# Sums of the gate's modulation moved from the merge stage into the stage of Strassen pairs

## The reference

```python
def modulation(cvec, w_ada, b_ada):
    mod = jax.nn.silu(cvec) @ w_ada + b_ada          # w_ada: 2048 x 6144
    shift, scale, gate = jnp.split(mod[:, None, :], 3, axis=-1)
...
    u = rmsnorm(x, norm_pre_w) * (1 + scale) + shift
    aq, ak, av, az, mq, mk, mv, mo, mz, mg, ga, gb = split_proj(u, w_in)
    ... windowed attention (branch B), mLSTM scans (branch A) ...
    merged = jax.nn.sigmoid(ga) * (y_a @ w_proj_a) + jax.nn.sigmoid(gb) * (y_b @ w_proj_b)
    out = rmsnorm(merged @ w_out, norm_post_w)
    return x + gate * out
```

## Time and profile before

| | |
|---|---|
| time, median of 3 runs | 1955.51 us (1955.37 to 1955.7) |
| the profiled execution: its own time | 1955.12 us |
| its span, first to last instruction | 1953.5 us |
| PE busy | 1920.3 us, 98% |
| DVE busy | 1204.0 us, 62% |
| ACT busy | 668.8 us, 34% |
| POOL busy | 113.2 us, 6% |
| mean granted clock of PE | 0.998 |

### The profile page before, as it was taken

How to read it: one execution, slowest core, us unless ns; L and a number is a source line. 1 busy time by engine, 2 the same in 40 slices (tenths; PEclk the granted TensorE clock), 3 DMA queues, 4 the chain that set the end, 5 groups by cost and what they waited for, 6 DMA issues and landing times.

```text
span 1953.5 us, 31682 instructions
## 1 busy us (share of the span) xinstructions
PE 1920.3 (98%) x12266; PEld 1782.6 (91%) x12266; DVE 1204.0 (62%) x2073; ACT 668.8 (34%) x1017; POOL 113.2 (6%) x201
## 2 busy tenths in 40 slices
PE   6999999999999999999999999999999999999998
PEld 2589999999999999999898999889889999988886
DVE  3368766666666666665766664465557767683224
ACT  4453333333333333332555554233224222242221
POOL 2010000000000000000000000000002000000000
PEclk9999999999999999999999999999999999999999
DMA  9962353333333333334632423355355666633224
GB/s 369 391 197 86 111 164 110 111 112 113 113 113 113 113 113 113 113 113 127 183 109 80 122 75 118 91 150 135 108 130 144 203 203 184 210 116 140 80 76 162
DMA packets 302319, 274.04 MB, mean 140 GB/s; under 512 B 20384, under 2 KB 253608, under 8 KB 300320
## 3 DMA queue, kind: packets, MB, share of 16 engines
q1 hardware_dynamic: 287984, 216.71, 37.9%
q0 software_dynamic: 13952, 56.00, 7.9%
q10 hardware_dynamic: 304, 0.25, 0.0%
HBM read 235.05 MB, written 40.48 MB: 141 GB/s over the span
## 4 chain that ended last, share of the span: by engine, by line
PE 91%; DVE 3%; DMA 3%; ACT 1%; issue 1%; SPq 1%; POOL 0%; DVEq 0%; POOLq 0%; ACTq 0%
PE bank L2060 20%; PE bank L2140 12%; PE bank L2133 12%; PE bank L2134 12%; PE bank L2356 11%; PE bank L2069 10%; PE bank L1973 2%; PE bank L2033 2%; PE bank L2260 2%; PE bank L2249 1%; PE bank L2201 1%; PE bank L2262 1%; PE bank L2178 1%; PE bank L2009 1%; DMA WORK<-in_w_ada_dram 1%
## 5 line engine op out<-in xcount | busy, mean ns | idle before, releaser
L2060 PE MATMUL bank<-XH,WH 128*128 128x320 f32 x1472 | 345.5, 316 | 2.8 <-DVE XL L1847 2.1
L1041 ACT ACTIVATE WH<-RAW 128x1024 fp32r<-128x1024 f32 x195 | 206.7, 1060 | 386.1 <-PE bank L2140 306.2
L2060 PE MATMUL bank<-XL,WH 128*128 128x320 f32 x1472 | 335.1, 309 | 0.0
L1482 DVE TENSOR_TENSOR WL<-RAW,WH 128x1024 fp32r<-128x1024 f32 x195 | 238.3, 1222 | 143.8 <-ACT WH L1041 143.8
L920 ACT ACTIVATE WH<-RAW 128x1024 fp32r<-128x1024 f32 x122 | 129.1, 1059 | 532.3 <-PE bank L2069 407.8
L2060 PEld LDWEIGHTS bank<-XH,WH 128*128 128x128 f32 x1472 | 244.5, 188 | 10.8 <-issue 8.0
L2060 PEld LDWEIGHTS bank<-XL,WH 128*128 128x128 f32 x1472 | 246.2, 188 | 0.0
L2069 PE MATMUL bank<-XH,WL 128*128 128x320 f32 x1472 | 235.9, 310 | 0.0
L2069 PEld LDWEIGHTS bank<-XH,WL 128*128 128x128 f32 x1472 | 220.0, 188 | 4.1 <-issue 3.8
L2134 PE MATMUL bank<-XL,WH 128*128 128x320 f32 x720 | 212.5, 309 | 0.0
L2133 PE MATMUL bank<-XH,WH 128*128 128x320 f32 x720 | 212.5, 309 | 0.0
(11 more groups left out here) (245 smaller groups left out, 2962.9 us busy)
## 6 DMA issues: line engine op xcount, KB each, us to landing
RAW<-in_w_in_dram SPq DMA_DIRECT2D x165, 512.0 KB, 3.8
WORK<-in_w_ada_dram SPq DMA_DIRECT2D x62, 512.0 KB, 5.4
proj_dram<-OUTS POOLq DMA_DIRECT2D x92, 320.0 KB, 2.5
RAW<-in_w_out_dram SPq DMA_DIRECT2D x32, 512.0 KB, 3.9
WORK<-proj_dram SPq DMA_DIRECT2D x16, 640.0 KB, 4.5
WORK<-proj_dram POOLq DMA_DIRECT2D x32, 320.0 KB, 3.3
RAW<-in_w_ada_dram SPq DMA_DIRECT2D x18, 512.0 KB, 9.3
RAW<-in_w_proj_a_dram SPq DMA_DIRECT2D x16, 512.0 KB, 4.7
```

The costliest lines, as they stand in the source:

```text
L1041: ins = nc.scalar.activation(WH[:, (j + p) % 2, :], pair_raw(j, p), ACT.Copy)
L1482: V.tensor_tensor(WL[:, w, :], pair_raw(j, p), WH[:, w, :].bitcast(F32), ALU.subtract)\
L2060: pe.matmul(banks[n][:, 0:HALF_TOK], wh[:, k, :], x[:, k0 + k, n * HALF_TOK:(n + 1) * HALF_TOK], start=(first and k == 0 and wi == 0), sto ...
```

## The change

The gate's sums move into the pair stage. `w_ada` is now taken in 64 pieces of 128 rows (one k-tile) by 512 columns, 256 KB each, loaded by POOL into four buffers (GAR). DVE adds each into GACC, which holds 512 columns for the two vectors: two instructions a step. The 16 steps of one column group fill 8 pairs; POOL then stores GACC to device memory (`gsum`, 512 KB), and the next group starts. Three groups lie in pairs 1 to 24 (two steps a pair); the fourth lies in the last five pairs with 4, 3, 3, 3 and 3 steps. The hardware loops of all engines now hold 8 pairs and run 3 times. In the merge stage SP's loads of `w_ada`, the memset and the 32 steps are gone; POOL loads the four stored sums back into GS, with `norm_post_w` and `b_ada`, and DVE adds `b_ada` to partition 0 in two instructions. WORK grows by 3000 words a partition, and the area of SBUF for the descriptors of POOL's DMAs is set to 4096 bytes a partition. A few semaphores of the start are merged into one (`setup`, and `m0_in` into `scan_in`).

```diff
+LOOP, LOOPS = 8, 3
+GADA_LAST = [4, 3, 3, 3, 3]
+assert 1 + LOOP * LOOPS + len(GADA_LAST) == PAIRS and sum(GADA_LAST) == KT
+WORK_WORDS = 14500
...
+    gsum = nc.dram_tensor("gsum_dram", (4 * P, 2 * 512), F32, kind="Internal").ap()
...
+        GACC = WORK[:, 11400:12424].rearrange("p (v n) -> p v n", v=2)
+        GAR = WORK[:, 12424:14472].rearrange("p (s n) -> p s n", s=4)
...
+        def gada_steps(j):
+            if j <= LOOP * LOOPS:
+                return range(2 * ((j - 1) % LOOP), 2 * ((j - 1) % LOOP) + 2)
+            n = j - LOOP * LOOPS - 1
+            return range(sum(GADA_LAST[:n]), sum(GADA_LAST[:n + 1]))
...
@@ SP, merge stage
-                        gada_load(i, 2 * k + x)
...
@@ POOL, pair stage
+            def gada_store(i, m):
+                pool.wait_ge(gada_used, 16 * i + 16 * (m + 1))
+                pool.dma_start(gsum[bass.ds(P * i + P * m, P), :], GACC.rearrange("p v n -> p (v n)")).then_inc(gacc_out, 16)
+                pool.wait_ge(gacc_out, 16 * i + 16 * (m + 1))
+                nc.gpsimd.tensor_tensor(ZERO[:, 7:8], ZERO[:, 0:1], ZERO[:, 0:1], ALU.add).then_inc(gacc_free, 1)
+            def gada_loads(i, m, steps):
+                for k in steps:
+                    if m or k >= 4:
+                        pool.wait_ge(gada_used, 16 * i + (16 * m + k - 3))
+                    pool.dma_start(GAR[:, k % 4, :], w_ada[0, k * P:(k + 1) * P, bass.ds(512 * i + 512 * m + 4096, 512)])\
+                        .then_inc(gada_in[k % 4], 16)
...
-            with pool.Fori(1, PAIRS_PLAIN // 2) as i:
-                for j in (1, 2):
-                    spill_pair(i, j, 4 * i + (T_PAIR + 2 * j + 2))
+            with pool.Fori(1, LOOPS) as i:
+                for j in range(1, LOOP + 1):
+                    if j < LOOP:
+                        gada_loads(i, 0, gada_steps(j + 1))
+                    else:
+                        gada_loads(i, 1, range(2))
+                        gada_store(i, 0)
+                    spill_pair(i, j, 2 * LOOP * i + (T_PAIR + 2 * j + 2))
+            for j in range(LOOP * LOOPS + 1, PAIRS):
+                if j == LOOP * LOOPS + 1:
+                    gada_loads(0, 3, range(2, GADA_LAST[0]))
+                if j + 1 < PAIRS:
+                    gada_loads(0, 3, gada_steps(j + 1))
+                else:
+                    gada_store(0, LOOPS)
+                spill_pair(0, j, T_PAIR + 2 * j + 2 if j < PAIRS_PLAIN else RB_GA + 2 * (j - PAIRS_PLAIN))
...
@@ POOL, merge stage
-            nc.gpsimd.memset(GS, 0.0).then_inc(filled, 1)
-            pool.wait_ge(filled, 4)
-            for v in range(2):
-                pool.dma_start(GS[0:1, v, :], b_ada[0:1, 4096:6144]).then_inc(gacc_init, 16)
+            pool.wait_ge(gacc_out, 16 * 4)
+            for m in range(4):
+                pool.dma_start(GS[:, :, 512 * m:512 * m + 512],
+                               gsum[m * P:(m + 1) * P, :].rearrange("p (v n) -> p v n", v=2)).then_inc(gs_in, 16)
+            pool.dma_start(NPW, norm_post_w[0].partition_broadcast(P)).then_inc(gs_in, 16)
+            pool.dma_start(GBIAS, b_ada[0:1, 4096:6144]).then_inc(gs_in, 16)
...
@@ DVE, pair stage
+            def gada_step(i, j, k):
+                m = 0 if j <= LOOP * LOOPS and not (isinstance(i, int) and j > LOOP) else LOOPS
+                dve.wait_ge(gada_in[k % 4], 64 * i + (64 * m + 16 * (k // 4 + 1)))
+                if k == 0:
+                    dve.wait_ge(gacc_free, i + (m + 1))
+                else:
+                    dve.wait_ge(gada_used, 16 * i + (16 * m + k))
+                for v in range(2):
+                    acc = GACC[:, v, :]
+                    col = VC[:, k + 16 * v:k + 16 * v + 1]
+                    if k == 0:
+                        ins = V.tensor_scalar(acc, GAR[:, 0, :], col, None, ALU.mult)
+                    else:
+                        ins = V.scalar_tensor_tensor(acc, GAR[:, k % 4, :], col, acc, ALU.mult, ALU.add)
+                ins.then_inc(gada_used, 1)
...
                 pair_lo(i, j, PR_S2)
...
+                if steps:
+                    gada_step(i, j, steps[0])
                 pair_lo(i, j, PR_S1)
...
                     pair_lo(i, j, PR_S3)
+                    gada_step(i, j, steps[1])
                     pair_lo(i, j, PR_S4)
+                    for k in steps[2:]:
+                        gada_step(i, j, k)
                 sums_b(i, j)
...
-            with dve.Fori(0, PAIRS // 2 - 1) as i:
-                for j in (1, 2):
+            with dve.Fori(0, LOOPS) as i:
+                for j in range(1, LOOP + 1):
...
@@ DVE, merge stage
-                    gada_step(i, 2 * u)
                     lo(i, 4, 2 * (T_MERGE + u) + 3)
-                    gada_step(i, 2 * u + 1)
...
+            dve.wait_ge(gs_in, 16 * 6)
+            for v in range(2):
+                ins = V.tensor_tensor(GS[0:1, v, :], GS[0:1, v, :], GBIAS, ALU.add)
+            ins.then_inc(gs_bias, 1)
...
@@ PE, pair stage
-            with pe.Fori(0, (PAIRS - 1) // 2) as i:
-                for j in (1, 2):
+            with pe.Fori(0, LOOPS) as i:
+                for j in range(1, LOOP + 1):
                     for p in range(7):
                         pair_product(i, j, p)
...
-    nc = _bacc.Bacc("TRN2", target_bir_lowering=False, num_devices=1)
+    nc = _bacc.Bacc("TRN2", target_bir_lowering=False, num_devices=1, dynamic_dma_scratch_size=4096)
```

More of the change, by code:

```diff
@@ L386, in hybrid_layer @@
         rows_in, const_in, x_in, aconst_in = sem("rows_in"), sem("const_in"), [sem(f"x_in{b}") for b in range(5)], sem("aconst_in")
-        m0_in, filled = sem("m0_in"), sem("filled")
+        filled = sem("filled")
         raw_in = [sem(f"raw_in{i}") for i in range(4)]
-        gada_in = [sem(f"gada_in{i}") for i in range(2)]
+        gada_in = [sem(f"gada_in{i}") for i in range(4)]
         start_in = [sem(f"start_in{i}") for i in range(START_RAW)]
@@ L565, in _ @@
             pair_pieces(T_PAIR, 0, P * (T_PAIR + 2), False)
[L566 to L571, removed]
+            with sp.Fori(0, LOOPS) as i:
+                for j in range(1, LOOP + 1):
+                    t = T_PAIR + 2 * j
+                    pair_pieces(t, 2 * LOOP * i, 2 * LOOP * P * i + P * (t + 2), j % 2 == 1)
+            for j in range(LOOP * LOOPS + 1, PAIRS):
+                t = T_PAIR + 2 * j
+                pair_pieces(t, 0, P * (t + 2) if j < PAIRS_PLAIN else COL_MERGE + 2 * P * (j - PAIRS_PLAIN), j % 2 == 1)
             def key_loads(g):
@@ L741, in _ @@
                         merge_half(i + 1, k, x)
-                        gada_load(i, 2 * k + x)
[L743 to L746, removed]
+            for q in range(8):
                 out_piece(0, q)
@@ L817, in spill_pair @@
             def spill_pair(i, j, row):
-                pool.wait_ge(sums, 12 * i + (6 * j + 6))
+                pool.wait_ge(sums, 6 * LOOP * i + (6 * j + 6))
                 pool.dma_start(proj[bass.ds(row * P, P), :], OUTS[:, 0, :]).then_inc(spilled[0], 16)
-                pool.wait_ge(out_ready, 4 * i + (T_PAIR + 2 * j + 2))
+                pool.wait_ge(out_ready, 2 * LOOP * i + (T_PAIR + 2 * j + 2))
                 pool.dma_start(proj[bass.ds(row * P + P, P), :], OUTS[:, 1, :]).then_inc(spilled[1], 16)
-            for j in range(3):
+            def gada_store(i, m):
[9 more added lines that the diff above has]
+                        .then_inc(gada_in[k % 4], 16)
+            gada_loads(0, 0, gada_steps(1))
+            spill_pair(0, 0, T_PAIR + 2)
+            for j in (1, 2):
+                gada_loads(0, 0, gada_steps(j + 1))
                 spill_pair(0, j, T_PAIR + 2 * j + 2)
@@ L939, in _ @@
             act.wait_ge(rows_in, 16 * 5)
-            nc.scalar.activation(OUTS[0:32, 0, 0:P], ROWS[0:32, :], ACT.Sigmoid).then_inc(silu_e, 1)
+            nc.scalar.activation(OUTS[0:32, 0, 0:P], ROWS[0:32, :], ACT.Sigmoid).then_inc(setup, 1)
             def start_hi_part(g):
@@ L1076, in _ @@
             pair(0, 0)
-            with act.Fori(0, PAIRS // 2 - 1) as i:
-                for j in (1, 2):
+            with act.Fori(0, LOOPS) as i:
+                for j in range(1, LOOP + 1):
                     pair(i, j)
-            for j in range(2 * (PAIRS // 2) - 1, PAIRS):
+            for j in range(LOOP * LOOPS + 1, PAIRS):
                 pair(0, j)
@@ L1866, in merge @@
                 V.tensor_tensor(Y[:, 2 * i + u, :], MT[:, 0, :], MT[:, 1, :], ALU.add).then_inc(merged, 1)
[L1868 to L1876, removed]
-                        ins = V.scalar_tensor_tensor(acc, AR[:, m % 2, 512 * k:512 * k + 512],
-                                                     VC[:, bass.ds(2 * i + (k + 16 * v), 1)], acc, ALU.mult, ALU.add)
-                    ins.then_inc(gada_used if k else gada_k, 1)
-            dve.wait_ge(gacc_init, 32)
             with dve.Fori(0, 7) as i:
@@ L2147, in _ @@
                 pair_product(0, 0, p)
-            with pe.Fori(0, (PAIRS - 1) // 2) as i:
-                for j in (1, 2):
```

(4 more changed lines are left out.)

84 lines of the change are left out of this document (39 added, 45 removed).

## The result

The changed kernel took 1964.3 us in the median of 6 runs (1961.52 to 1968.02); the kernel before took 1955.47 us beside it. The ratio is 1.0046, with a 95% interval of 1.0033 to 1.0059. I had forecast 1955.6 us, in a range of 1954.0 to 1959.5, with 0.12 for slower: wrong. The profiled execution is the longest of the six: span 1966.5 us, 13.0 more than before.

What follows compares the result with a forecast made beforehand. PE bounds the kernel, busy 1920.3 of 1953.5 us. Merge, gaps, POOL and transfers each add 0, so the span stays 1953.5 and the median 1955.5, said as 1955.6 us for losses left open; range 1954.0 to 1959.5.

Steps and rivals of the forecast that it cites:

- instruction fetch at the loop's edge: Rival, pair stage: PE must fetch at two jumps back, up to 3.7 us each, 0 to 7.4 us; chance 0.15.
- the cover: Loop's edge: PE's sequencer may be up to 4 us ahead of the array; then a jump's fetch shows nothing.
- Nothing back from the merge stage: Merge stage: taking 95 us from DVE and 16 MB of loads from SP gains 0; PE idles 0.0 us there.
- The sums fit into DVE's gaps: Pair stage: two steps of 1.5 us each fit DVE's idle 1.89 and 2.06 us in a pair; cost 0.
- POOL's queue: Pair stage: two added loads a pair take 1.1 us of POOL's 20.56 us idle before the first store; cost 0.
- Transfers: Pair stage: 26 GB/s more beside 115 GB/s, with 4.5 us left for the tightest loads; cost 0.

Runs made afterwards that it cites:

- a_again: The changed kernel as it is, run again for a second profile: 1963.38 us against 1955.76 of the kernel before, ratio 1.0041.
- a_more: The changed kernel as it is, run once more for a third profile: 1963.05 us against 1956.28 of the kernel before, ratio 1.0036.
- b_pe8: The kernel before with only PE's loop changed to eight pairs and three rounds, no sum moved: 1962.69 us against 1955.52, ratio 1.0038.
- b_pe6: The kernel before with only PE's loop changed to six pairs and four rounds: 1970.74 us against 1955.76, ratio 1.0075.
- b_pe8_more: The kernel before with PE's loop of eight pairs and no sum moved, run once more: 1963.98 us against 1956.28, ratio 1.0042.

## Why the prediction was wrong, by its own steps

**What failed** is the rival "instruction fetch at the loop's edge", which I priced at 0 for the sum and gave 0.15. Its mechanism, its two jumps and its bound (3.7 us each) stood in the text, and 7.06 us came of a bound of 7.4. That the two figures are so near is chance: the bound was two whole fetches of one block each, and the 7.06 are two shorter stalls at each jump and a lower clock behind one. The step that failed is the cover: "PE's sequencer needs nothing new after the wait for low A22 [...] so it may be up to 4 us ahead of the array; then nothing shows". The q8 packet at 402 us and the array's end at 403.86 show a lead of 1 to 2 us; when the fetch was asked for, and so the whole lead, no row shows. PE went on at 405.82, 2.8 to 3.8 us after that packet began, so even from there the fetch took about what I had priced for all of it, 3.7 us, and the lead hid only part: 1.5 to 2.3 us of idle PE were left at every one of the fourteen jumps. And I priced one block a jump; there are two that show. The 3.0 us and 1.2 us that I added up tell when the weights are ready and how long the pass is; no row showed how far the sequencer runs ahead, while the earlier trace rows both stood for the stall; with the Trainium skill's figure for PE's memory beside the 2688 instructions of the body, this should have been the likeliest case. My sentence that by the page's rule the old body fits takes PE's whole memory for the window; the runs bear that out, but the page speaks of two pages.

**The clock** I had left out. A stall of PE can cost more than itself: behind the first jump of the profiled execution twelve matmuls at 0.27 us instead of 0.147 took about 1.4 us more. In the net it was less. From the low pass before the jump to the next low pass (starts 402.52 and 410.18, 603.68 and 610.09) the first jump took 7.66 us and the second, without a fall, 6.41, where the passes otherwise follow each 3.52 us: 4.1 us lost against 2.9. The second of each two starts is in these rows:

```profile
410.18 1.34 PE L2186 MATMUL bank<-XH,WL 128*128 128x320 f32 x8
...
610.09 1.34 PE L2186 MATMUL bank<-XH,WL 128*128 128x320 f32 x8
```

**Nothing back from the merge stage**: right (PE 214.00 of 214.00). DVE's busy time fell by 76 us there, from 160.16 to 84.17, and not by about 90: of the 95 us of sums only 82.4 lay between 1500 and 1716 us, and the two additions are new. The two additions of `b_ada` took 4.47 us, where I had 4.9 from twice the length:

```profile
1711.98 4.47 DVE L1941 TENSOR_TENSOR WORK<-WORK 1x2048 f32<-1x2048 f32 x2
```

**The sums fit into DVE's gaps**: right. A pair of the changed kernel away from the jumps, which answers to the earlier trace rows:

```profile
663.27 1.41 DVE L1607 SCALAR_TENSOR_TENSOR WORK<-WORK,VC 128x512 f32<-128x512 f32 x2
665.33 1.23 DVE L1524 TENSOR_TENSOR WL<-RAW,WH 128x1024 fp32r<-128x1024 f32 x1 [0.65 <-ACT WH L1083]
...
670.23 1.41 DVE L1607 SCALAR_TENSOR_TENSOR WORK<-WORK,VC 128x512 f32<-128x512 f32 x2
672.37 1.23 DVE L1524 TENSOR_TENSOR WL<-RAW,WH 128x1024 fp32r<-128x1024 f32 x1 [0.73 <-ACT WH L1083]
```

The idle times before low S1 and low S4 fell from 1.89 and 2.06 to 0.65 and 0.73 us; I had 0.4 and 0.6.

**POOL's queue**: right. The store of a finished group, POOL's instruction behind it and the first store of OUTS, just ahead of the second jump:

```profile
595.56 0.55 POOL L833 DMA_DIRECT2D gsum_dram<-WORK  x1 [11.92 <-DVE WORK L1607]
598.86 0.19 POOL L835 TENSOR_TENSOR ZERO<-ZERO 128x1 f32<-128x1 f32 x1 [2.75 <-DMA gsum_dram<-WORK]
602.82 0.58 POOL L826 DMA_DIRECT2D proj_dram<-OUTS  x1 [3.77 <-DVE OUTS L1568]
```

POOL was free 3.8 us before the store of OUTS could go. Its instruction took 0.19 us, where I allowed 1.20.

**Transfers**: 139 GB/s in the pair stage where I had 115 + 26 = 141, and nothing lost by it.

## What to carry to other kernels

When an edit makes a hardware loop's body longer, count the instructions of the busiest engine in it, and look whether the trace shows instruction fetches inside the loop as it is: none in the old loop and one every 20 us in straight code meant that the body was held, and that a longer one might not be. An engine that isn't part of the edit can keep its own loop: here PE's loop of two pairs beside DVE's of eight gives the time of before. A body that is too long costs more the shorter it is, since it jumps more often (13.9 us for six pairs, 6.7 for eight, 4.15 for fourteen); writing the loop out cost nothing here.

The move itself is free and gains nothing, because PE waited for nobody in the merge stage. In a kernel bound by PE, taking load off another engine in a stage is worth at most what PE idles there.

## What the runs showed of the hardware that I had not expected

- A jump back to a part of the program that is no longer held stopped PE for 1.5 to 2.3 us, and in thirteen of fourteen jumps once more, for 0.25 to 1.7 us, each time twelve matmuls later, behind the next block of 16 KB.
- a_again had 5.2 us of idle PE at its two jumps and a_more 5.3, the first profile 4.8; their pair stages, 746.5, 746.6 and 746.1 us, lost 7.1 to 7.6. Most of the remainder is the lower clock, which each of them had at one of its jumps. In b_pe8 the clock never fell in the pair stage, and 5.8 us of idle time cost 6.7: the idle time of a row counts from the end of a matmul 0.31 us long, while matmuls start every 0.147, so each of the four stretches costs 0.16 us more than its row says.
- PE's granted clock fell to 0.50 after some of the idle stretches (1.78 and 2.15 us in b_pe6) and not after others (2.31 us in b_pe8_more left it at 1.00). It fell at six of the fourteen jumps, and the length of the stretch doesn't tell which.
